# Attention's output projection as three products of rounded parts, with its weights split during the query projections and the softmax loop

## The reference

```python
def attend(q, k, v):
    s = jnp.einsum('bqhgd,bkhd->bhgqk', q, k).astype(jnp.float32) * (HEAD_DIM ** -0.5)
    p = jax.nn.softmax(s, axis=-1).astype(v.dtype)
    return jnp.einsum('bhgqk,bkhd->bqhgd', p, v)

def attention_mixer(h_lat, h_ctx, w_qkv, g_q, g_k, w_o, need_ctx_out):
    ...
    o_blocks = lax.map(lambda qblk: attend(qblk, k_all, v_all), qb)
    o_lat = o_blocks.transpose(1, 0, 2, 3, 4, 5).reshape(B, L, D) @ w_o
...
        x = x + gt1 * rms_norm_2(y_lat, g_mix_post[i])
        m_lat = sq_relu_mlp(modulate(rms_norm_2(x, g_mlp_pre[i]), sh2, sc2), w_mlp_in[i], w_mlp_out[i])
        x = x + gt2 * rms_norm_2(m_lat, g_mlp_post[i])
```

## Time and profile before

| | us |
|---|---|
| median of 3 runs | 1927.43 |
| lowest and highest | 1927.14, 1929.66 |
| the profiled execution's own time | 1927.07 |
| its span, first to last instruction | 1925.3 |
| its mean granted TensorE clock | 0.956 |

### The profile page before, as it was taken

One profiled execution on the slowest core, in us unless ns is written; L12 is line 12 of the kernel. 1 busy time (PEld: TensorE's weight loads), 2 busy tenths in 40 slices (PEclk: granted clock), 3 DMA queues, 4 the chain that ended last, 5 costly groups with the idle time before them and its releaser, 6 DMA issues.

```text
span 1925.3 us, 26004 instructions
## 1 busy us (share of the span) xinstructions
PE 1670.9 (87%) x10812; PEld 1103.2 (57%) x10812; DVE 800.3 (42%) x1232; ACT 504.9 (26%) x762; POOL 29.6 (2%) x27
## 2 busy tenths in 40 slices
PE   8999877688788689998788888857689999999998
PEld 7877433245344258775343453422279995548997
DVE  6696312011111046884201110120177775637676
ACT  6434212000000044342100000121264433444342
POOL 0000000000000000000000000000030000000000
PEclk9999988899999999999999999989899999999999
DMA  9887899999999999758999999999945563325451
GB/s 371 298 302 305 352 427 424 421 426 423 421 425 420 428 404 336 284 234 358 428 423 422 425 420 425 425 427 424 409 179 182 198 230 131 131 69 194 174 187 53
DMA packets 127607, 626.58 MB, mean 325 GB/s; under 512 B 7315, under 2 KB 9747, under 8 KB 102294
## 3 DMA queue, kind: packets, MB, share of 16 engines
q1 hardware_dynamic: 126930, 624.86, 80.9%
q10 hardware_dynamic: 580, 0.33, 0.1%
HBM read 622.02 MB, written 3.15 MB: 325 GB/s over the span
## 4 chain that ended last, share of the span: by engine, by line
PE 51%; DMA 33%; DVE 11%; ACT 3%; issue 1%; SPq 1%; DVEq 0%; POOL 0%; ACTq 0%
DMA ring<-in_w_up 16%; DMA ring<-in_w_mlp_in 9%; PE bank L593 8%; PE bank L595 8%; PE bank L594 8%; DMA ring<-in_w_mlp_out 6%; PE bank L1168 6%; PE bank L1186 5%; PE bank L1029 5%; DVE w_low L494 3%; PE bank L1417 2%; PE bank L1534 1%; DMA ring<-in_w_down 1%; PE bank L1064 1%; DVE hgrn_diag L494 1%
## 5 line engine op out<-in xcount | busy, mean ns | idle before, releaser
L1029 PE MATMUL bank<-ring,xeT 128*32 128x512 f32 x1920 | 264.8, 698 | 109.6 <-DMA ring<-in_w_up 109.3
L1029 PEld LDWEIGHTS bank<-ring,xeT 128*32 128x32 f32 x1920 | 68.8, 120 | 292.3 <-issue 291.8
L494 ACT ACTIVATE silu_g<-bank 128x256 f32<-128x256 f32 x32 | 12.3, 383 | 691.3 <-PE bank L1029 691.3
L494 DVE TENSOR_TENSOR hid_e<-silu_g,bank 128x256 f32<-128x256 f32 x32 | 13.5, 421 | 376.7 <-ACT silu_g L494 376.7
L2656 DVE TENSOR_TENSOR w_low<-ring,w_high 128x1024 fp32r<-128x1024 f32 x128 | 153.5, 1241 | 9.8 <-ACT w_high L1938 5.3
L1938 ACT ACTIVATE w_high<-ring 128x1024 fp32r<-128x1024 f32 x128 | 126.5, 1049 | 85.0 <-PE bank L595 85.0
L593 PE MATMUL bank<-x_high,w_high 128*128 128x256 f32 x512 | 145.1, 283 | 3.2 <-DVE x_low L494 2.9
L594 PE MATMUL bank<-x_low,w_high 128*128 128x256 f32 x512 | 144.8, 283 | 0.0
L595 PE MATMUL bank<-x_high,w_low 128*128 128x256 f32 x512 | 144.6, 283 | 0.0
L1186 PE MATMUL bank<-ring,ctx_hid 128*128 128x512 f32 x256 | 121.7, 637 | 24.0 <-DMA ring<-in_w_mlp_out 24.0
L1168 PE MATMUL bank<-ctx_xT,ring 128*128 128x256 f32 x512 | 120.6, 399 | 24.0 <-DMA ring<-in_w_mlp_in 24.0
(11 more groups left out here) (285 smaller groups left out, 2558.2 us busy)
## 6 DMA issues: line engine op xcount, KB each, us to landing
ring<-in_w_down SPq DMA_DIRECT2D x60, 2048.0 KB, 30.1
ring<-in_w_up SPq DMA_DIRECT2D x60, 2048.0 KB, 24.4
ring<-in_w_gate SPq DMA_DIRECT2D x60, 2048.0 KB, 21.8
ring<-in_w_ada SPq DMA_DIRECT2D x24, 2048.0 KB, 11.5
ring<-in_w_mlp_in SPq DMA_DIRECT2D x24, 2048.0 KB, 8.5
ring<-in_w_mlp_out SPq DMA_DIRECT2D x24, 2048.0 KB, 7.9
ring<-in_w_in SPq DMA_DIRECT2D x16, 2048.0 KB, 10.3
ring<-in_w_out SPq DMA_DIRECT2D x4, 2048.0 KB, 7.7
```

Of the source, the lines that this page charges most:

```text
L494: self.ins, self.mine = op(*args, **kw), "none"
L1029: ins = mm(ps[32 * j:32 * j + 32, :], xeT[:, g % 2, c, i * CAP:(i + 1) * CAP], w[:, :, k, j, :, :], start=c == 0, stop=c == KC - 1, skip_g ...
```

## The change

The output projection uses `product` in place of the plain matmul. For that:

- **Heads are split as they finish.** ACT copies a head from its PSUM bank to `o_high` (`values_high`: in even steps from 2 on, after the exponentials of step u + 1 and ahead of the `probT` copy of step u). DVE then waits for it and writes `o_low` as the bank minus `o_high`, where it copied to `oT` before.
- **The weights of the first half (n = 0)** are split during the query projections of tile 0 (ACT, all four quarters; DVE two of them) and in steps 3 and 6 of the softmax loop (DVE, the other two).
- **The weights of the second half (n = 1)** are split by ACT in steps 5, 7, 9 and 11 ahead of the `probT` copy of that step, and by DVE at the end of steps 9 and 12 and, for the last two quarters, after the loop.
- **The MLP's first weights** use the place of w_o's first high part, so their split moves from the end of the loop to between the two tiles: ACT starts it when PE has finished half n = 0 of tile 1; DVE does three quarters ahead of tile 1's `gate_banks` and the fourth between the two halves of `split_modulated`.
- PE waits for `wo_low_ready` at every second piece of tile 0.

```diff
+WO_HIGH_AT = (5, 7, 9, 11)
+WO_LOW_AT = {3: (0, 2), 6: (0, 3), 9: (1, 0), 12: (1, 1)}
...
-                    ins = mm(ps[:, :], oT[:, c, t * P:(t + 1) * P], w[:, c, :], start=c == 0,
-                             stop=c == KC - 1)
+                    if t == 0 and c % 2 == 0:
+                        pe.wait_ge(S_("wo_low_ready"), 4 * n + c // 2 + 1)
+                    part = slice(t * P, (t + 1) * P)
+                    ins = product(ps[:, :], (o_high[:, o_at(c), part], o_low[:, c, part]),
+                                  (wh[:, c, :], wl[:, c, :]), c == 0, c == KC - 1)
...
+            f(high[:, quarter(q)], whole[:, quarter(q)], ACT.Copy).then_inc(
+                S_("wo_high_ready"), 1)
...
+        def values_high(head):
+
+            name = ("o", head)
+            ps = full(act, name)
+            f(o_high[:, o_at(head), :], ps[:, 0:S], ACT.Copy).then_inc(S_("o_high_ready"), 1)
+
...
+                if t == 0:
+                    for q in (2 * n, 2 * n + 1):
+                        wo_high(0, q)
...
+            if u >= 2 and u % 2 == 0:
+                values_high(u // 2 - 1)
+            if u in WO_HIGH_AT:
+                wo_high(1, WO_HIGH_AT.index(u))
             name = ("pT", u)
...
-        first_high(1)
+        values_high(NQ - 1)
...
             if t == 0:
                 row_of("rows_mlp1", 0, 1)
+                mlp_high(1, 0, 0, range(4), items[("mix2", 1, 3)][1] + 1)
...
+        def wo_low(n, q):
+
+            dve.wait_ge(S_("wo_high_ready"), 4 * n + q + 1)
+            whole, high, low = (w[:, quarter(q)] for w in wo_parts(n))
+            tt(low, whole, high.bitcast(F32), ALU.subtract).then_inc(S_("wo_low_ready"), 1)
...
-            free(copy(oT[:, head, :], ps[:, 0:S]), name)
+            expect("o_high_ready")
+            free(tt(o_low[:, head, :], ps[:, 0:S], o_high[:, o_at(head), :].bitcast(F32),
+                    ALU.subtract), name)
...
+            if u in WO_LOW_AT:
+                wo_low(*WO_LOW_AT[u])
         take_values(NQ - 1)
-        first_low(1)
+        for q in (2, 3):
+            wo_low(1, q)
...
+            if t:
+                mlp_low(1, 0, 0, (0, 1, 2))
```

More of the change, by code:

```diff
@@ L294, in build_program @@
     q_raw = place("q_raw", [P, NT, D], where="x_full")
-    oT = place("oT", [P, NQ, S], where="x_full")
+    o_high = place("o_high", [P, NQ, S], F32R, where="xT2")
+    o_low = place("o_low", [P, NQ, S], F32R, where="x_full")
     at[0] = here["consts_sb"] + 4 * CONSTS["decay"][0]
@@ L307, in build_program, with o_at, wo_parts @@
     output_plan = {0: (0, 1), 1: (2, 3)}
+    def o_at(head):
+        return (head + NQ // 2) % NQ
+    def wo_parts(n):
+        slot = items[("mix2", 1, 3 + n)][0]
+        return ring[:, slot, :], w_high[:, n, :], w_low[:, slot, :]
     def quarter(q):
@@ L1527, in _ @@
                 it = ("mix2", 1, 3 + n)
-                w = wait_landed(pe, it).rearrange("p (c n) -> p c n", c=KC)
+                wh, wl = (w.rearrange("p (c n) -> p c n", c=KC) for w in wo_parts(n)[1:])
                 name = ("wo", n, t)
@@ L2006, in _, with wo_high @@
         row_of("rows_mix1", 0, 0)
+        def wo_high(n, q):
+            if q == 0:
+                slot, _, value = items[("mix2", 1, 3 + n)]
+                act.wait_ge(landed[slot], value)
+            if (n, q) == (0, 0):
+                act.wait_ge(weights_used, items[("mlp", 0, 15)][1] + 1)
+            whole, high, _ = wo_parts(n)
+            f(high[:, quarter(q)], whole[:, quarter(q)], ACT.Copy).then_inc(
[4 more added lines that the diff above has]
+            f(o_high[:, o_at(head), :], ps[:, 0:S], ACT.Copy).then_inc(S_("o_high_ready"), 1)
         for t in range(NT):
@@ L2819, in _ @@
         q_rows(0, 0)
+        wo_low(0, 0)
         q_rows(0, 1)
+        wo_low(0, 1)
         k_rows(1)
@@ L2858, in _, with between @@
             normalise_x4(t, 1)
-        split_modulated("xm1", 1, lambda: last_bias(3))
+        def between():
+            last_bias(3)
+            mlp_low(1, 0, 0, (3,))
+        split_modulated("xm1", 1, between)
         dve.wait_ge(S_("ys_cleared"), 2)
```

## The result

| | before | the change |
|---|---|---|
| median, 22 runs each | 1927.68 us | 1932.15 us |
| lowest to highest | 1926.28 to 1930.09 | 1929.01 to 1935.6 |
| ratio, 95% interval | | 1.0024 (1.0018 to 1.0030) |
| the profiled execution's span | 1925.3 us | 1933.4 us |

The change makes the kernel 0.24% slower. The direction and the range of the forecast hold (1929.4, range 1925.3 to 1932.4), its size does not: +2.0 us were forecast, +4.5 came. That is beyond the 0.2% (3.9 us) within which the forecast had put 76% of its chances; slower than that had 18%.

A forecast was written before the change was run, and what follows sets the result against it. The prediction took a ring of PE, ACT and DVE to bound the softmax loop, with the projection following unbroken. Projection -5.16 and loop +7.2 gave +2.0 us on 1927.07, so 1929.1; with 0.36 for the median 1929.4, range 1925.3 to 1932.4.

The forecast's parts named there:

- Part 1: Output projection, both tiles: 96 products at 0.2323 us take 22.30 us instead of 27.46, a gain of 5.16 us.
- Part 2: Heads' split in the softmax loop: DVE's subtraction starts 0.42 us later, 0.36 us a pair in pairs that DVE bounds.
- Parts 3 and 4: w_o's quarters in the loop: +1.11 us for pairs with ACT's steps 5, 9, 11; +1.57 for DVE's steps 6, 12.
- Part 5: Splits moved to the query projections and between the tiles: hidden in waits, cost 0, at most 0.5 us for the fourth quarter.
- rival B: PE's clock falls in the loop: up to 1.6 us a stretch, 1931.0 us with one, 1932.6 with two; 15%.
- Part 4: w_o's low parts on DVE: steps 6 and 12 +1.57 us each, steps 3 and 9 0, at most 0.5 each.
- A: Moved work in the loop is mostly hidden: 1925.2 us, or 1922.3 with everything hidden; 15%.
- C: Projection's products cost less than in the MLP, 0.116 us each: projection 11.2 us, kernel 1918.3 us; 1%.
- D: Projection's products wait for parts, tile 0 stalling for the last quarters; needs a delay over 5 us; 2%.

The follow-up runs named there:

- the fillers: The change plus 13 small matmuls, results unread, in PE's pauses of the softmax loop: +2.7 us against the kernel before (ratio 1.0015), +3.4 us (1.0017) when repeated.

## Why the prediction was right and wrong

**Part 1, the projection: right.** 5.16 us were summed, 4.96 came (29.27 to 24.31). The products stand 0.232 us apart as in the MLP; the two tiles' first ones need 0.4 and 0.6 us, which the sum left out. The Trainium skill's 131 ns ("TensorE: Matmul & The Clock Gate", "Back-to-back issue gap") are not met here either.

**Part 2, the heads: right.** 5.08 to 5.14 us a pair forecast, 5.13 with the quarters gone. The experiment with the heads one pair later takes 3.4 us out of the loop at full clock (42.4 to 39.0).

**Parts 3 and 4, the quarters: right, a little small.** 5.83 and 6.29 us a pair were summed, 5.84 to 5.90 and 6.46 came. A single quarter costs 1.06 us on ACT and 1.23 on DVE; the 0.97 and 1.16 that I took are means of four in a row. At full clock the loop is 42.4 us, 7.4 more than before against 7.2 forecast. That the sum comes so near is in part luck: it counts every pair from 4.72 us, but (6,7) took 5.02 before, which takes 0.3 us off the difference, and the pairs came out some 0.5 us longer in all than summed. Why (6,7) took 5.02 no run was made to tell.

**Part 5, what moved elsewhere: right.** The MLP starts 8.87 us behind the projection, as before. Its fourth quarter took 2.03 us on DVE beside POOL, hidden as forecast:

```profile
1744.14 1.28 POOL L506 TENSOR_TENSOR x_low<-x_full,x_high 128x512 fp32r<-128x512 f32 x1 [130.43 <-ACT x_high L506]
...
1744.47 2.03 DVE L2697 TENSOR_TENSOR w_low<-ring,w_high 128x1024 fp32r<-128x1024 f32 x1
```

The cover on ACT held as well. Its copies began 0.64 us after it was idle, and it still waited 0.72 us for the last product (half a microsecond was forecast); the square of tile 1's second half starts 0.11 us behind the projection's end, as before:

```profile
1730.14 3.91 ACT L1953 ACTIVATE w_high<-ring 128x1024 fp32r<-128x1024 f32 x4 [0.64 <-PE bank L607]
...
1735.67 0.60 ACT L506 ACTIVATE xs<-bank 128x512 f32<-128x512 f32 x1 [0.72 <-PE bank L607]
```

**The sum: too small by rival B.** By the terms the kernel should be 7.4 - 5.0 = 2.4 us slower. The two falls of the clock add 3.0 us in the profiled executions, and the medians are 4.5 and 5.0 up. The step that failed is that the sum puts the clock in the loop at nothing: that loss stands in rival B alone, with "The loop itself ran at full clock before. 15%.", and Part 4 prices steps 6 and 12 alike. Both quarters hold the scaling of the next step up by the same 1.2 us; but behind step 12 PE has no scores left, and the pause becomes 3.2 us of transposes alone. The case was in the earlier trace rows, at the loop's entry. B's own price for two stretches, 1932.6, is near the time that came (1932.15). Its size for a stretch, "up to 1.6 us", measures 1.42 and 1.54 on the values of heads 6 and 7. That the range still held, with 0.25 us to spare, is luck: it was drawn to leave two such stretches out.

**Rivals.** A is out (no pair stayed near 4.7). C and D are out too: the projection took 24.3 us without a stall. The account and the clock are both shown by experiments: the order of the work by those that move it, and the cost of the falls by the fillers, which add work and take time away, and by the quarter of step 12. What exactly in the pause lets the clock fall is not shown.

**What stays open.** The second fall follows the values of head 6 and a pause of the same kind between steps 14 and 15; but the kernel without step 12's quarter has that pause too, and no fall in it:

```profile
1700.87 1.03 PE L1517 MATMUL bank<-probT,ctx_v 128*128 128x256 f32 x4
1701.73 0.60 PE L1505 MATMUL bank<-consts_sb,prob 128*128 128x128 f32 x4
1703.67 0.66 PE L1505 MATMUL bank<-consts_sb,prob 128*128 128x128 f32 x4 [1.34 <-DVE prob L506]
1705.06 1.10 PE L1517 MATMUL bank<-probT,kv 128*128 128x256 f32 x4 [0.73 <-issue]
```

From 1701.90 to 1705.06 that is 3.2 us too, with eight transposes (1.26 us) where the first fall had four (0.66). The kernels with no quarters in the loop and with the low quarters out have the same pause and no fall either. So the first fall seems to be needed for the second, and the length of a pause alone does not decide; no run tells more.

What the falls cost in the medians is open as well. Between the change and the fillers it is 1.7 and 1.6 us, each against the kernel before beside it or on one chip, where the profiles give 3.0; in the kernel without high quarters the median is 2.1 us below what the profile gives. But between the kernels without step 6's and without step 12's quarter the medians differ by 4.5 us and the loops in the profiles by 3.9. Perhaps not every execution has both falls, but with one profile for each kernel run that is only argued.

## What to carry to other kernels

In a ring of three engines look for the instruction that stands ahead of the next critical one in its engine's order, not only for the one whose result is late: here the copy of a finished head, which PE needed up to 30 us later, stood on the path, and splitting each head one pair later took 3.4 us out of the loop. Preparation may be put into such a loop only in a slot in which its engine waits for something else that takes longer, and the same work one step later can be free. And ask of each pause that is made longer what TensorE has left in it: here 3.2 us with only four transposes were followed by a fall of the clock, and a delay of 1.2 us cost some 4.5.

## What the runs showed of the hardware that was not expected

- Adding 13 matmuls to a loop made it 3.0 us shorter, as the clock stayed at 2.4 GHz (45.4 and 45.5 us without, 42.4 and 42.4 with them).
- In all four profiles in which step 12's quarter follows a head's split that waits for ACT, and no fillers stand in the loop, the clock fell at the same two places, within 1.2 us (34.0 to 35.2 and 41.0 to 42.0 us behind the first values); in the other nine profiles never in the loop. The longest stretch of transposes and waits without a fall was 3.2 us too, with eight transposes instead of four (between the values of heads 6 and 7 in the kernels without step 12's quarter, without low quarters and with no quarters in the loop).
- A copy of 128 x 1024 on ACT is 1.06 us alone and 0.97 in a row of four; the subtraction on DVE 1.23 and 1.16.
